# RG-LRU stage: gate projection first, decays three blocks behind the convolution, roots and scans beside the merge

## What is computed

```python
xc = conv4(xr) + conv_b                                   # depthwise, 4 taps
r = sigmoid(heads(xc) @ w_a + b_a)                        # 16 heads of 64
i = sigmoid(heads(xc) @ w_x + b_x)
log_a = -LRU_C * r * softplus(-lam);  a = exp(log_a)
b_in = sqrt(-expm1(2.0 * log_a)) * (i * xc)
h = scan(a, b_in)                                         # h[t] = a[t] h[t-1] + b_in[t]
y_c = h * gelu(rg)
merged = gates[0] * (y_a @ w_br_a) + gates[1] * (y_b @ w_br_b) + gates[2] * (y_c @ w_br_c)
x = x + rms_norm(merged @ w_o, g_post_mix)
```

## Time and profile before

| | us |
|---|---|
| median of the runs | 3152.57 |
| the profiled execution, its own time | 3153.24 |
| its span | 3151.5 |
| PE busy | 2905.2 (92%) |
| DVE busy | 1480.7 |
| ACT busy | 1241.5 |
| stretch from the end of nsa to w_o | 485.8 to 896.1 |

### The profile page before, as it was taken

How to read it: one execution, slowest core, us unless ns; L and a number is a source line. 1 busy time by engine, 2 the same in 40 slices (tenths; PEclk the granted TensorE clock), 3 DMA queues, 4 the chain that set the end, 5 groups by cost and what they waited for, 6 DMA issues and landing times. The chain is left out here.

```text
span 3151.5 us, 56646 instructions
## 1 busy us (share of the span) xinstructions
PE 2905.2 (92%) x24856; PEld 2342.5 (74%) x24856; DVE 1480.7 (47%) x2298; ACT 1241.5 (39%) x2080; POOL 458.0 (15%) x346
## 2 busy tenths in 40 slices
PE   7799999699999999898889998788999999889999
PEld 5687556588877888775578887576888888778887
DVE  2332776533344333436553344765555555454343
ACT  3222564422233222325543233554445554443232
POOL 1101452000000000112200000002434444100000
PEclk9898999899999999999999999898999999999999
DMA  4121002133222222232122222220000000322221
GB/s 164 58 95 67 15 1 74 55 119 107 94 80 107 87 107 94 76 118 72 66 94 94 94 107 71 97 79 15 7 7 7 7 5 6 109 89 97 97 100 67
DMA packets 38821, 228.84 MB, mean 73 GB/s; under 512 B 4352, under 2 KB 8448, under 8 KB 15024
## 3 DMA queue, kind: packets, MB, share of 16 engines
q1 hardware_dynamic: 32576, 201.34, 17.8%
q0 software_dynamic: 6000, 23.87, 2.2%
HBM read 220.93 MB, written 4.26 MB: 71 GB/s over the span
## 5 line engine op out<-in xcount | busy, mean ns | idle before, releaser
L431 DVE TENSOR_TENSOR weights_lo<-ring,weights_hi 128x1024 fp32r<-128x1024 f32 x341 | 421.7, 1238 | 716.3 <-ACT weights_hi L424 716.1
L424 ACT ACTIVATE weights_hi<-ring 128x1024 fp32r<-128x1024 f32 x364 | 382.1, 1054 | 607.1 <-PE bank L561 360.4
L480 PE MATMUL bank<-h_hi,weights_hi 128*128 128x512 f32 x512 | 207.6, 406 | 53.9 <-DVE weights_lo L431 33.0
L481 PE MATMUL bank<-h_lo,weights_hi 128*128 128x512 f32 x512 | 206.0, 402 | 0.0
L482 PE MATMUL bank<-h_hi,weights_lo 128*128 128x512 f32 x512 | 205.2, 401 | 0.0
L480 PE MATMUL bank<-mlp_h_hi,weights_hi 128*128 128x512 f32 x512 | 200.9, 392 | 2.0 <-DVE mlp_h_lo L776 2.0
L481 PE MATMUL bank<-mlp_h_lo,weights_hi 128*128 128x512 f32 x512 | 200.6, 392 | 0.0
L482 PE MATMUL bank<-mlp_h_hi,weights_lo 128*128 128x512 f32 x512 | 200.4, 391 | 0.0
L559 PE MATMUL bank<-weights_hi,mlp_p_hi 128*128 128x512 f32 x512 | 199.4, 389 | 0.0
L561 PE MATMUL bank<-weights_hi,mlp_p_lo 128*128 128x512 f32 x512 | 199.2, 389 | 0.0
L560 PE MATMUL bank<-weights_lo,mlp_p_hi 128*128 128x512 f32 x512 | 199.2, 389 | 0.0
(11 more groups left out here) (487 smaller groups left out, 6282.5 us busy)
## 6 DMA issues: line engine op xcount, KB each, us to landing
ring<-in_w_m SPq DMA_DIRECT2D x64, 1024.0 KB, 4.5
ring<-in_w_mb SPq DMA_DIRECT2D x24, 1024.0 KB, 4.6
ring<-in_w_fi SPq DMA_DIRECT2D x22, 1024.0 KB, 4.6
ring<-in_w_fo SPq DMA_DIRECT2D x10, 1024.0 KB, 4.7
ring<-in_w_a SPq DMA_DIRECT2D x7, 1024.0 KB, 4.8
attn_bias<-scratch POOLq DMA_DIRECT2D x16, 448.0 KB, 4.6
ring<-in_w_rg SPq DMA_DIRECT2D x5, 1024.0 KB, 4.9
ring<-in_w_v SPq DMA_DIRECT2D x4, 1024.0 KB, 14.4
```

Of the source, the lines that this page charges most:

```text
L424: act.e.activation(halves(g, s)[0], raw, ACT.Copy).then_inc(*act.up("act_unit_high", ("high", s)))
L431: lane.e.tensor_tensor(lo, raw, hi.bitcast(F32), ALU.subtract).then_inc(*lane.up(f"{lane.name}_unit_low", ("low", s)))
L480: pe.e.matmul(ps[:, :], hi, xh, start=k == 0, stop=False, skip_group_check=True)
L481: pe.e.matmul(ps[:, :], hi, xl, start=False, stop=False, skip_group_check=True)
```

## The change

The order of the two projections is swapped and the work around them is laid out anew:

- `w_rg` is streamed and multiplied first. Its first two weight units are split during the last attention job, in places freed by a new assignment of the attention's transposed tiles (`PT`), and PE has no fence after nsa.
- The gate matmuls become pairs of 64x64 ones, one pair for each block and gate, without the zero blocks (POOL's two memsets go). The pair of block nb-2 stands right behind block nb of w_xr; that of block 7 stands in the merge, behind its first block.
- Sigmoid becomes Tanh of half the argument, with the factors folded in (`hb`, c8 = -4 softplus). The square a^2 moves from DVE to ACT. In step i of w_xr ACT makes the gates of block i-3 and the decay of block i-4.
- Roots (ACT) and scans (DVE) move into `w_mb0`, steps 1 to 6.
- Each branch has its own low halves, written over the branch itself, and the high halves have two areas in turn. So the halves of a branch are made during the `w_mb` before: two per gate block in the second half of `w_mb0`, one per gate block in `w_mb1` and `w_mb2`.
- POOL splits no units here any more; the reload of x waits for the last scan.

The core of the diff (lines of the removed order are to be seen in the functions above):

```diff
-          ("w_vt", 4096), ("w_xr", 8192), ("w_rg", 8192)]
+          ("w_vt", 4096), ("w_rg", 8192), ("w_xr", 8192)]
...
-    L.ys = pair("y", W1, NB * S)
+    high = [area(f"y_hi{j}", at, NB * S, F32R) for j, at in enumerate((W1 + 2 * NB * S, W1))]
+    low = [area(f"y_lo{j}", at, NB * S, F32R) for j, at in enumerate([W0 + c * NB * S for c in (2, 3, 4)] + [W1 + NB * S])]
+    L.ys = [[high[c % 2], low[c]] for c in range(4)]
...
 def act_nsa(g, act):
+        if n == len(NSA_JOBS) - 1:
+            act.wait_ge(g.at("pt_read", n - 1, 2))
+            act_unit(g, act, first_units("w_rg")[0])
...
+def pe_gates(g, pe, nb):
+    L = g.L1
+    pe.wait_ge(g.at("diagonals"))
+    pe.wait_ge(g.at("conv", nb))
+    for j, w in enumerate((L.bda, L.bdx)):
+        ps = bank(g, pe, ("ri", nb, j))
+        for par in range(2):
+            half = slice(64 * par, 64 * par + 64)
+            m = pe.e.matmul(ps[half, :], w[half, nb, :], L.xc[half, nb, :], start=True, stop=True, skip_group_check=True)
+        m.then_inc(*pe.up("pe_ri", ("filled", ("ri", nb, j))))
...
+    g.rotating, g.turn = ROT, HEADS_ROT
     pe_gemm(g, pe, "w_rg", NB, range(NB), part_of(L.hs), lambda nb, k: ())
+    pe_gemm(g, pe, "w_xr", NB, range(NB), part_of(L.hs), lambda nb, k: (), after=after)
+    pe_gates(g, pe, NB - 2)
...
+def act_decay(g, act, nb):
+    c8 = L.c8[:, nb:nb + 1]
+    act.wait_ge(g.at("c8"))
+    act.wait_ge(g.at("gated_x", nb))
+    act.e.activation(L.ii[:, nb, :], L.rr[:, nb, :], ACT.Tanh, scale=c8, bias=c8).then_inc(*act.up("act_decay"))
+    act.wait_ge(act.newest)
+    act.e.activation(L.rr[:, nb, :], L.rr[:, nb, :], ACT.Exp, scale=c8, bias=c8).then_inc(*act.up("act_decay"))
+    act.wait_ge(act.newest)
+    if nb:
+        act.wait_ge(g.at("one_minus", nb - 1))
+    act.e.activation(L.a2, L.rr[:, nb, :], ACT.Square).then_inc(*act.up("act_decay", ("decay", nb)))
...
+    for what, i in gemm_steps("w_xr", NB, range(NB)):
+        if what == "unit":
+            act_unit(g, act, i)
+            continue
+        if i >= 3:
+            act_gates(g, act, i - 3)
+        if i >= 2:
+            act.wait_ge(g.at("conv", i - 2))
+        act.e.activation(L.xs[i % 2][:, 3:S + 3], filled(g, act, ("w_xr", i))[:, :], ACT.Copy).then_inc(
+            *act.up("act_xs", ("xs", i), ("drained", ("w_xr", i))))
+        if i >= 4:
+            act_decay(g, act, i - 4)
...
+def branch_halves(c, n):
+    if c == 0:
+        return (2 * n - 8, 2 * n - 7) if n >= 4 else ()
+    return (n,) if c == 1 else (n - 1,) if n else ()
...
 def act_merge(g, act):
+            if c == 0 and i == 1:
+                act_gates(g, act, NB - 1)
+                act_decay(g, act, NB - 2)
+                act_decay(g, act, NB - 1)
+            if c == 0 and i == 2:
+                act_roots(g, act)
+                act_gate(g, act, 0, 0)
+            if i % 2 == 0 and (c or i):
+                act_gate(g, act, c, i // 2)
+                for k in branch_halves(c, i // 2):
+                    act_branch(g, act, c + 1, k)
...
 def dve_merge(g, dve):
+    scans = {2: (0, 1, 2), 3: (3,), 4: (4, 5), 6: (6, 7)}
...
+            for nb in scans.get(i, ()) if c == 0 else ():
+                dve_recurrence(g, dve, nb)
```

More of the change, by code:

```diff
@@ L45 @@
 RAW = ("wk1", "wv1")
-GROUPS = (("w_v", "w_u"), ("w_q", "w_kv"), ("w_vt",), ("w_xr", "w_rg"), ("w_mb0", "w_mb1", "w_mb2", "w_o"),
+GROUPS = (("w_v", "w_u"), ("w_q", "w_kv"), ("w_vt",), ("w_rg", "w_xr", "w_mb0", "w_mb1", "w_mb2", "w_o"),
           ("w_fi0", "w_fo0", "w_fi1", "w_fo1"), ("w_a2",), ("w_va",), ("w_ao",), ("w_m100", "w_m200", "w_m101", "w_m201"),
@@ L244, in memory @@
     a = Shelf("nsa_heads", SLOT0, 6 * UNIT)
+    L.PT = [a.take(S) for _ in range(4)]
+    late = [a.take(S) for _ in range(2)]
+    L.PT += [a.take(S) for _ in range(2)] + [L.yC[:, j, :] for j in range(4, 8)] + late
+    a.take(UNIT)
     L.PC = [a.take(S) for _ in range(2)]
-    L.PT = [L.yC[:, j, :] for j in range(4, 8)] + [a.take(S) for _ in range(NSA_SLOTS - 4)]
+    assert SPLIT0["w_rg"] % 3 == 0
     L.Pc = L.yC[:, 0:4, :].rearrange("p a b -> p (a b)")[:, 0:QT * 16 * NCMP].rearrange(
@@ L1363, in dve_nsa @@
             dve_nsa_narrow(g, dve, n + 1)
+        else:
+            low_unit(g, dve, first_units("w_rg")[0])
         for i in range(3):
@@ L1409, in act_rglru @@
     fence(g, act, "nsa")
-    for s in first_units("w_xr"):
-        act_unit(g, act, s)
+    act_unit(g, act, first_units("w_rg")[2])
     act.wait_ge(g.at("lam_low"))
     act.e.activation(L.sp_t[:, 1, :], L.sp_t[:, 0, :], ACT.Exp).then_inc(*act.up("act_lam", ("lam_exp",)))
[L1414 to L1427, removed]
     for what, i in gemm_steps("w_rg", NB, range(NB)):
@@ L1501, in dve_rglru @@
     fence(g, dve, "nsa")
+    low_unit(g, dve, first_units("w_rg")[2])
     dve_lam(g, dve)
+    for what, i in gemm_steps("w_rg", NB, range(NB)):
+        if what == "unit":
+            low_unit(g, dve, i)
+            continue
+        low_part(g, dve, ("y", 0, i), L.yA[:, i, :], cols(L.ys[0], i))
     for what, i in gemm_steps("w_xr", NB, range(NB)):
@@ L1514, in dve_rglru @@
         dve.mark("conv", i)
[L1515 to L1531, removed]
-            dve.e.tensor_tensor(L.yC[:, m, :], L.gl[:, m, :], L.ii[:, m, :], ALU.mult).then_inc(*dve.up("dve_rglru"))
+        if i >= 4:
+            dve_one_minus(g, dve, i - 4)
+    for nb in (NB - 3, NB - 2):
+        dve_gated(g, dve, nb)
+        dve_one_minus(g, dve, nb - 1)
     end(g, dve, "rglru")
@@ L1569, in act_merge, with act_gate @@
+def act_gate(g, act, c, n):
+    if c or n >= 2:
+        act.wait_ge(g.at("gate_read", *((c, n - 2) if n >= 2 else (c - 1, NB - 2 + n))))
+    key = (f"w_mb{c}", 2 * n)
+    act.e.activation(g.L1.gt[n % 2], filled(g, act, key)[:, :], ACT.Sigmoid).then_inc(*act.up("act_gate", ("gate", c, n), ("drained", key)))
 def act_merge(g, act):
     L = g.L1
-    fence(g, act, "rglru")
-    for s in first_units("w_mb0"):
-        act_unit(g, act, s)
-    for k in range(NB):
-        high_part(g, act, ("y", 0, k), L.yA[:, k, :], cols(L.ys, k))
@@ L1576, in act_merge @@
     for c in range(3):
-        name = f"w_mb{c}"
-        for what, i in gemm_steps(name, NB, range(2 * NB)):
+        for what, i in gemm_steps(f"w_mb{c}", NB, range(2 * NB)):
             if what == "unit":
                 act_unit(g, act, i)
-            elif i % 2 == 0:
-                n = i // 2
-                if c or n >= 2:
-                    act.wait_ge(g.at("gate_read", *((c, n - 2) if n >= 2 else (c - 1, NB - 2 + n))))
-                act.e.activation(L.gt[n % 2], filled(g, act, (name, i))[:, :], ACT.Sigmoid).then_inc(
-                    *act.up("act_gate", ("gate", c, n), ("drained", (name, i))))
```

187 lines of the change are left out of this document (105 added, 82 removed).

## The result

Seen together on one chip, the changed kernel took 3105.95 us (median of 4 runs, 3102.96 to 3107.57) and the kernel before 3153.9 (4 runs, 3150.43 to 3156.46): a ratio of 0.9847, 95% interval 0.9835 to 0.9859. The profiled execution took 3105.51 us, where 3105 was forecast.

What follows compares the result with a forecast made beforehand. PE bounds the kernel, losing 49.84 us between nsa's end and w_o to late weight and y halves and slow matmuls. From 3153.24, all that back less 1.8 for the gates gives 3105.2, said as 3105; range 3101 to 3119.

Steps and rivals of the forecast that it cites:

- The four losses: PE's lost time between nsa's end and w_o, all to come back: start 6.52, w_rg 29.92, merge 8.36, w_o 5.04 us.
- The start: First projection behind nsa: splitting its first units inside the last attention job was to take back the whole 6.52 us.
- the last y: Start of w_o: only the last eighth of y remains when w_mb2 ends, so all 5.04 us were to come back.
- the stall in w_rg: w_rg took 73.44 us for 43.52 of matmuls, at clock 0.81; all 29.92 us lost were to come back.
- The gates' price: Gate matmuls as 16 pairs of 64x64 instead of 16 full-size: 1.8 us extra, bounds 0 and 15.1.
- 0.2 per place, 1.4 in all: Change of shape at seven gate places: a full-size fp32 matmul between pairs takes 1.06 us instead of 0.86.
- the first rival: The two halves of each gate pair run in turn: 15.1 us spent on gates, 3118.5 in all; chance 6%.
- Spare time at unit 5: In w_mb0, DVE's low half of unit 5 is ready at 28.9 and PE asks at 32.8: 3.9 us to spare.
- the second rival: A new PE wait of 1 to 8 us in w_xr or w_mb0, giving 3106 to 3115; chance 16%.
- The table loads: A load of 1.28 us stands before ACT's roots in w_mb0; ACT_TABLE_LOAD was to appear four times instead of eight.
- The returning stall: PE waits 2 to 4 us in each of 8 w_xr steps, so 16 to 32 go: 3121 to 3137; chance 6%.
- 1.2 GHz through w_xr: Small gate matmuls in 7 places drop PE to half speed in w_xr and gates: 59 us more, 3164; chance 2%.

Runs made afterwards that it cites:

- e4: Changed kernel with the first three units of w_rg split behind nsa instead of two of them inside its last attention job: 3111.93 us.
- e3: Changed kernel with the last branch's y halves made all eight behind w_mb2 instead of one behind each gate block: 3112.05 us.
- e5: Changed kernel with all eight decays in step 1 of w_mb0 instead of one per step of w_xr from the fourth on: 3119.72 us.
- e1: Changed kernel with all eight recurrences in step 2 of w_mb0 on DVE, instead of three, one, two and two: 3121.9 us.
- e7: Changed kernel with gates 0 to 3 as full-size fp32 matmuls on block-diagonal weights, gates 4 to 7 still pairs: 3103.16 us, one run.
- e11: Changed kernel with the same gate pairs set in four places of w_xr and the merge instead of seven: 3104.66 us, one run.
- e2: Changed kernel with four recurrences instead of three in step 2 of w_mb0 and none in step 3: 3106.33 us, one run.

## Why the prediction was right

The sum was 49.84 us back less 1.8 for the gates, 48.0; the stage gave 47.28.

- **The four losses, 49.84.** All came back: no wait from 483.27 to w_o, and clock 1.00. Two were brought back alone. The start is worth 5.62 of its 6.52 (e4), and the last y 6.35 where 5.04 stood (e3). The order of decays and scans, which the prediction put at the stall in w_rg and at w_mb, is worth 12.7 (e5) and 12.65 (e1), now all in `w_mb0`. These are not parts of 49.84: both act on unit 5's 2.9 us to spare, so undone together they need not add up. No run undoes the swap of w_rg and w_xr by itself, so what the swap is worth apart from the places of decays and scans is not shown.
- **The gates' price, 1.8, was mis-sized: it is 2.67.** The first w_rg matmul to the first of w_o is 847.97 - 483.27 = 364.70 us; 1536 matmuls between at 0.2267 are 348.16, so 16.54 is left. The first three matmuls took 0.14 more than their 0.68 (483.27 to 484.09), which leaves 16.4 for the gates against 13.73 before. The step that failed is "0.2 per place, 1.4 in all", with the half-way guess for the pairs' own excess. It measured the other way round: the pairs cost nothing over full-size matmuls (0.86 each), and a place costs 0.36, 2.5 for seven (e7, e11). The 0.90 came from the earlier trace rows pairs of 128 columns; at 512 columns the excess is gone, and no run shows where it went. By e7, full-size matmuls in all seven places would save an estimated 2.2 us (7 at 0.32): the pairs are a small loss in time. The Trainium skill, *TensorEngine Tiling (Array Packing)*, Restrictions and Gotchas, says that different row tiles cannot access the same PSUM bank at the same time, by which the two halves would run in turn. This trace disagrees, with 3.58 us for four pairs where in turn it would be about twice that. So the first rival is out.
- **Spare time at unit 5: 2.9 us, not 3.9.** A recurrence with its two products is 2.66 us and not 2.5 (its first product starts at 603.79 and the next one's at 606.45), some 0.5 for three; the first root ends at 601.0, 20.0 behind 581.01 and not 19.6, which is 0.4 more. The sum doesn't hang on it, but e2 and e1 show how near it was: one recurrence more fits, with 0.25 us left. A second would not, by this sum; the runs show the second rival's wait for five.
- **The table loads.** The roots start 1.29 us behind the load's start (599.17, 600.46), as the prediction reckoned from the earlier trace rows. The 2.66 that the Trainium skill, *ScalarE: Activation LUTs*, What ACT_TABLE_LOAD costs, gives for a switch with its drain doesn't show there.
- **"The returning stall" and "1.2 GHz through w_xr"** did not occur: ACT is busy 40.29 of the 68.19 us of the stretch with w_xr and the gates, DVE 43.56, and the granted clock is 1.00.
- **The 3105.2 itself** was met to 0.3 us in the profiled execution partly by luck: the stage gave 0.7 less than forecast, the time ahead of it 2.6 more and the time behind took back 2.1. The term "later phases are the same" holds to some 2 us, not to tenths.

## What to carry to other kernels

When a matmul engine waits for a prepared operand that had landed long ago, look at what stands ahead of the preparation in the preparing engine's program, and give every such piece a place in a stretch where the matmul engine has more to do than the others; compute the slack at each operand, since it is the smallest one that decides (here 2.9 us, and one recurrence more fits, five cost 12.7). Count a wait at more than its length: where a wait of 3 to 11 us could be read alone here, the matmuls at the lower clock level behind it cost another 1.7 to 3.0 us. And compare variants in a stretch between two events of the trace: it repeated to 0.1 us where whole runs of the changed kernel spread over 4.6.

## What the hardware showed beyond expectation

- Two 64x64 fp32 matmuls of 512 columns on opposite quarters, into the two halves of one bank, take the 0.86 us of one 128x128: six pairs 5.29 us, four 3.58, two 1.86. In the trace's records the matmuls of the two halves start within 0.01 us of each other, and the next two 0.43 to 0.48 us later: they run side by side. Going to such pairs and back costs 0.36 us a time, where a full-size fp32 matmul in the same place costs 0.04.
- The time ahead of the stage differs from kernel to kernel though its instructions are the same: w_rg starts between 482.05 and 487.85 in the changed kernel and its variants with that part unedited (less the 3.23 us wait in e4). Of the 4.6 us between the changed kernel and e1_scans8, 1.3 are there already when PE's wait of 4.16 us ends (243.62 and 244.96); the rest lies behind it, where the granted clock is below 1.00 in both and lower in e1_scans8. Windows of PE there, in the changed kernel and in e1_scans8, laid 1.34 us apart:

```profile
283.62:303.62 20.00, 18.50 (x179) 0.84 0.28 106
303.62:323.62 20.00, 20.00 (x89) 0.90 0.15 54
```

```profile
284.96:304.96 20.00, 18.23 (x167) 0.76 0.28 106
304.96:324.96 20.00, 20.00 (x86) 0.81 0.16 54
```

What makes the clock rise earlier in one and later in the other is open; no run here was made for it.
